# First modulation slot issued ahead of all else, recurrence masks loaded as bytes, positions worked on behind that slot

## The reference

```python
c_act = jax.nn.silu(c)
for l in range(DEPTH):                                  # DEPTH = 2
    mod = c_act @ w_mod[l] + b_mod[l]                   # (2048) @ (2048, 6144)
    shift, scale, gate = jnp.split(mod, 3, axis=-1)
    h = rmsnorm(x, norm_gain[l]) * (1.0 + scale[:, None, :]) + shift[:, None, :]
    proj = h @ w_in[l]
    ...
    att = sparse_attention(..., positions, rel_bias)    # bias = rel_bias[t5_bucket(pos_q - pos_k)]
    ...
    x = x + gate[:, None, :] * y
# second block: hgrn2_chunked over the rows, with causal masks inside each chunk
```

## Time and profile before

| | |
|---|---|
| median of 3 runs | 1891.88 us (1891.06 to 1892.19) |
| the profiled execution, its own time | 1894.75 us |
| its span in the profile | 1892.9 us |
| TensorE busy | 1851.9 us (98%) |
| VectorE, ScalarE, GpSimd busy | 71%, 52%, 11% |
| TensorE's share of the chain that ended last | 92% |
| mean granted TensorE clock | 0.988 |

### The profile page before, as it was taken

The page is one execution under the profiler, slowest core; times in us unless marked ns, Lnnn a source line. Parts: engine busy times, 40 slices in busy tenths (PEclk is TensorE's granted clock), DMA queues, the critical chain, the costliest instruction groups (busy, mean ns, idle before and its releaser), DMA issues.

```text
span 1892.9 us, 23983 instructions
## 1 busy us (share of the span) xinstructions
PE 1851.9 (98%) x9008; PEld 1535.2 (81%) x9008; DVE 1352.2 (71%) x1950; ACT 991.6 (52%) x1359; POOL 201.8 (11%) x256
## 2 busy tenths in 40 slices
PE   5989999999999999999999999999999999999997
PEld 3778788888888878888888888888888888888886
DVE  5988999989987778857765544487775456665555
ACT  6664555446446445544654644566665444444464
POOL 0000002100000000210000000044431020031001
PEclk9879999999999999999999999999999999999999
DMA  9998978975986986744465555654445555556552
GB/s 332 363 345 299 335 253 290 314 242 172 328 299 231 360 276 222 244 157 156 125 223 180 190 188 198 196 164 153 154 160 173 188 191 178 185 186 252 178 191 98
DMA packets 211825, 424.28 MB, mean 224 GB/s; under 512 B 7681, under 2 KB 12557, under 8 KB 210317
## 3 DMA queue, kind: packets, MB, share of 16 engines
q1 hardware_dynamic: 209788, 415.18, 64.6%
q10 hardware_dynamic: 1936, 7.76, 1.0%
HBM read 418.70 MB, written 4.21 MB: 223 GB/s over the span
## 4 chain that ended last, share of the span: by engine, by line
PE 92%; ACT 3%; DMA 2%; DVE 2%; issue 1%; SPq 0%; DVEq 0%; POOLq 0%; POOL 0%; ACTq 0%
PE acc L684 27%; PE acc L686 27%; PE acc L685 27%; DMA raw<-in_w_in 1%; PE sps L1075 1%; DVE scr L2076 1%; PE tps L725 1%; ACT w_hi L1414 1%; DMA xres<-in_x 1%; PE tps L765 1%; PE sps L790 0%; PE sps L892 0%; PE sps L893 0%; PE sps L996 0%; PE tps L988 0%
## 5 line engine op out<-in xcount | busy, mean ns | idle before, releaser
L1855 DVE TENSOR_TENSOR w_lo<-raw,w_hi 128x1024 fp32r<-128x1024 f32 (+1 forms) x580 | 720.8, 1249 | 461.3 <-ACT w_hi L1242 459.2
L1242 ACT ACTIVATE w_hi<-raw 128x1024 fp32r<-128x1024 f32 (+1 forms) x580 | 606.9, 1051 | 771.6 <-PE acc L686 693.8
L684 PE MATMUL acc<-w_hi,ht_hi 128*128 128x512 f32 (+1 forms) x2304 | 910.2, 395 | 0.5 <-issue 0.4
L686 PE MATMUL acc<-w_hi,ht_lo 128*128 128x512 f32 (+1 forms) x2304 | 894.1, 388 | 0.0
L685 PE MATMUL acc<-w_lo,ht_hi 128*128 128x512 f32 (+1 forms) x2304 | 892.3, 387 | 0.0
L686 PEld LDWEIGHTS acc<-w_hi,ht_lo 128*128 128x128 f32 x2304 | 432.4, 188 | 90.4
L684 PEld LDWEIGHTS acc<-w_hi,ht_hi 128*128 128x128 f32 x2304 | 432.9, 188 | 86.8 <-issue 2.6
L685 PEld LDWEIGHTS acc<-w_lo,ht_hi 128*128 128x128 f32 x2304 | 433.3, 188 | 83.4
L1987 DVE SCALAR_TENSOR_TENSOR scr<-raw,vcol,scr 128x512 f32<-128x512 f32 x154 | 110.9, 762 | 5.1 <-DVE w_lo L1855 0.5
L2076 DVE SCALAR_TENSOR_TENSOR scr<-raw,vcol,scr 128x1024 f32<-128x1024 f32 x56 | 68.2, 1279 | 6.9 <-DMA raw<-in_w_mod 6.9
L1987 DVE SCALAR_TENSOR_TENSOR proj<-raw,vcol,proj 128x512 f32<-128x512 f32 x70 | 52.3, 788 | 1.9
(11 more groups left out here) (304 smaller groups left out, 1480.3 us busy)
## 6 DMA issues: line engine op xcount, KB each, us to landing
raw<-in_w_in SPq DMA_DIRECT2D x208, 1024.0 KB, 5.1
raw<-in_w_mod SPq DMA_DIRECT2D x64, 1024.0 KB, 6.2
raw<-in_w_mod SPq DMA_DIRECT2D x64, 512.0 KB, 6.7
raw<-in_w_out SPq DMA_DIRECT2D x32, 1024.0 KB, 5.2
raw<-in_w_o SPq DMA_DIRECT2D x16, 1024.0 KB, 5.1
raw<-in_w_ple_gate SPq DMA_DIRECT2D x16, 1024.0 KB, 5.1
raw<-in_w_b_out SPq DMA_DIRECT2D x8, 1024.0 KB, 5.1
raw<-in_w_a_out SPq DMA_DIRECT2D x8, 1024.0 KB, 5.0
```

The source lines that it names most:

```text
L684: pe.matmul(o, hi_m, w_hi[:, slot, u, 0:width], start=start, stop=False)
L686: mm = pe.matmul(o, lo_m, w_hi[:, slot, u, 0:width], start=False, stop=stop)
L1242: act.activation(w_hi[:, x % SPL, :, 0:width], raw[:, j, 2 * (x % halves):2 * (x % halves) + 2, 0:width], ACT.Copy).then_inc(hi_ready, 1)
L1855: dve.tensor_tensor(w_lo[:, x % SPL, :, 0:width], raw[:, j, 2 * (x % halves):2 * (x % halves) + 2, 0:width], w_hi[:, x % SPL, :, 0:width]. ...
```

## The change

SP issues `mod_pair(0, 0)` first, then `consts` and `c`, then `mod_pair(0, 1)`. `levels` is handed over as an array of bytes, is loaded straight into `lvm`, and its transfer stands after the four quarters. VectorE's copy into `lvm` goes; a wait for the masks is put ahead of the recurrence. VectorE's work on positions moves from ahead of the first slot's `modulate` to behind it.

```diff
-    return k, lv
+    return k, lv.astype(np.uint8)
...
+            mod_pair(0, 0)
             sp.dma_start(kst[:, :], consts).then_inc(s_const, 16)
             vector_rows("c", c, s_c)
-            for j in range(2):
-                mod_pair(0, j)
+            mod_pair(0, 1)
             sp.dma_start(xres[:, :, :], x_rows).then_inc(s_x, 16)
...
             for j in range(2, RAW):
                 mod_pair(0, j)
-            sp.dma_start(scr[:, 5376:6016], levels.rearrange("p n t -> p (n t)")).then_inc(s_levels, 16)
...
+            sp.dma_start(lvm[:, :, :], levels).then_inc(s_levels, 16)
             for l in range(DEPTH):
...
-            dve.wait_ge(s_pos, 48)
-            dve.tensor_copy(prow, prow_i)
-            link(dve.tensor_copy(pcol, pcol_i))
...
+            def distances():
+
+                dve.wait_ge(s_pos, 48)
+                dve.tensor_copy(prow, prow_i)
+                link(dve.tensor_copy(pcol, pcol_i))
...
-            def bound_and_levels():
+            def bound_ratio():
                 dve.wait_ge(vec_ready, 2)
                 lp = v2("lb_param_2", 0, NH)
                 dve.tensor_tensor(lb_t[:, 0, :], lp, lp, ALU.subtract).then_inc(lb_stats, 1)
-                dve.wait_ge(s_levels, 16)
-                dve.tensor_copy(lvm[:, :, :], scr[:, 5376:6016].rearrange("p (n t) -> p n t", t=P))
-
-            dve.wait_ge(vec_ready, 1)
...
             dve.wait_ge(mod_summed, m_free.next(2))
+            dve.wait_ge(vec_ready, 1)
             for u in range(2):
                 modulate(0, 0, u)
+            distances()
...
                 if col == GATES:
+                    dve.wait_ge(s_levels, 16)
                     link(dve.memset(hat, 0.0))
```

More of the change, by code:

```diff
@@ L1945, in _ @@
             dve.memset(rb_diag, 0.0).then_inc(rb_zeroed, 1)
-            dve.wait_ge(s_pos, 48)
-            dve.tensor_copy(prow, prow_i)
-            link(dve.tensor_copy(pcol, pcol_i))
[L1949 to L1954, removed]
+            def distances():
+                dve.wait_ge(s_pos, 48)
+                dve.tensor_copy(prow, prow_i)
+                link(dve.tensor_copy(pcol, pcol_i))
+                for m in range(M):
+                    o, q = (slice(0, S), slice(0, S)) if m == 0 else (slice(S, 384), slice(P, S))
+                    r = dve.tensor_scalar(rel[:, o], prow[:, q], pcol[:, m:m + 1], None, ALU.subtract)
+                r.then_inc(rel_ready, 1)
+                dve.wait_ge(rel_ready, 1)
+                dve.tensor_scalar(bucket, rel, 0.0, float(EXACT), ALU.max, ALU.min).then_inc(clip_ready, 1)
             def buckets():
@@ L2100, in _ @@
                     if i == 0 and j == 6:
-                        bound_and_levels()
+                        bound_ratio()
                 dve.wait_ge(raw_read, own.ahead(0))
```

## The result

The changed kernel takes 1897.28 us (median of 6, 1896.07 to 1899.51) against 1891.59 for the one before (median of 6, 1891.01 to 1894.64): a ratio of 1.0027, 95% interval 1.0016 to 1.0037, so 3.0 to 7.0 us slower. A second set of runs gave 1.0026 (1.0016 to 1.0036). The forecast was 1893.2, with a range up to 1896.4.

The account below looks back on a forecast made before the run. TensorE is 98% busy, so only the head before full matmuls could move, paced by ScalarE's chain: +1.24 us for late squares, masks and copy 0, rounded to +1.3, giving 1893.2 us, range 1890.6 to 1896.4.

Parts of the forecast that it names:

- The bound and the way a delay is passed on: Head before full matmuls: ScalarE's chain sets `w_hi` at 41.77; the stream's earlier gain is lost as idle DMA.
- One for one: Head: what ScalarE's chain loses or gains before 41.77 us moves the end of the kernel equally.
- Masks and VectorE's copy: Stream and VectorE in the head: 0.83 us less stream and 0.49 us less copy, both worth nothing.
- S: Time VectorE can start the first slot, needing the slot and silu(c): taken as 8.2 us, bounds 6.7 and 12.4.
- the middle estimate: First slot lands at 7.7 us and `c` at 8.35, so VectorE can start the slot at 8.95.
- The price of S = 6.96 and beyond: ScalarE's squares: past 6.96 us they wait for signs, not x; a start at 8.2 costs 1.24 us.
- Signs start at S + 2.47: ScalarE's signs follow the first slot's two instructions (1.42 us) and the positions work (1.05 us).
- The buckets: VectorE, behind the signs: about 1.4 us later, from 16.79 to 18.2, with the third slot's wait as cover.
- Rival 3: Head: `c` held behind the slot until 10.2 or more, costing 3.8 us, up to 1897.3 at S = 12.4; chance 0.09.
- Rival 1: Head: no net effect, S at or under 7.2, signs end under cover of x; 1891.6 to 1892.2; chance 0.15.
- rival 2: Head: the stream's gain reaches the end, -1.5 us, 1890.4, if ScalarE's chain does not set 41.77; chance 0.10.
- Rival 4: TensorE's clock behind the head: low stretch changes length, 2.8 us less or more, 1889.1 to 1896.0; chance 0.06.

Follow-up runs that it names:

- held and ahead: Changed kernel with GpSimd's 3.60 us copy started only after VectorE clips the distances, and positions back ahead of the first slot: 1.0002 against the kernel before.
- changed kernel, again: The changed kernel, unaltered, timed once more against the kernel before on the same chip: 1.0026, +4.8 us.
- copy held: Changed kernel with a small identity tile made first and GpSimd's 3.60 us copy started only after VectorE clips the distances: 1.0014, +2.5 us against the kernel before.
- behind only: Kernel before with only VectorE's positions work moved behind the first slot; transfer order and masks as before: 1.0010, +1.9 us against the kernel before.

## Why the prediction was wrong

**The bound and the way a delay is passed on: right in kind.** ScalarE's squares set `w_hi`; in all fourteen profiles `w_hi` stands 24.6 us behind the squares to 0.05. The stream's gain was lost at 45 to 50, as said. "One for one" to the end is neither confirmed nor excluded: over the eight runs with late squares (from "held and ahead" to "changed kernel, again", 26.5 us of lateness in all) the medians gained 21.6, so 0.8 us for each, and the ratios give 23.3, so 0.9. The first set has 5.7 us for 5.31. Each of these times is uncertain by 1.7 us to either side. The first full matmul came 2.7 us later than in the first profile of the kernel before, and 3.7 to 4.8 later than in the second; it stands 116.3 to 119.0 us behind the squares in the fourteen profiles.

**Masks and VectorE's copy: right.** No effect found.

**S, the start of the first slot: mis-sized.** I took 8.2 and measured 9.93 and 10.16; the middle estimate was 8.95. The order of events was right: silu(c) is what it waits for. The constants took 9.09 - 1.82 = 7.3 us to be seen, `c` 7.0. SP's own issues also grew, `c` from 0.42 to 0.97. The pace was lower too: from 3 to 5 us the changed kernel moved 249 to 279 GB/s, where the estimates took 1 MB in 2.59 us. What held it there no run shows. By the prediction's own sum S = 9.93 puts the squares at 20.12 in place of 18.4, so this term was short by 1.7 us.

**The price of S = 6.96 and beyond: wrong by a term that was missing.** This is the step that failed, and the larger one. "Signs start at S + 2.47" took 1.42 us for the two instructions of the slot. They took 3.96. I had followed GpSimd's copy to 11.1 us for what waits for it, and had not asked what it does to VectorE beside it, though the estimate itself put both in the same stretch. So signs start at S + 4.93 = 14.86, 2.46 later than S alone would have it. The two terms together, 1.7 and 2.5, make up, to 0.1, the 4.07 us between the squares' forecast place of 18.41 and their measured 22.48.

Put in the order in which the runs take them away, the lateness of the squares is: GpSimd's copy beside VectorE 2.20 (changed kernel again, less copy held); positions behind the slot 2.01 (less held and ahead); positions landing late 1.03 (what is left). These add up to 5.24. In time the same steps are 2.4, 2.4 and 0.1 us, each with an uncertainty of over 1.

The last share depends on that order. With the positions behind the slot, as in the changed kernel, VectorE comes to them at 13.81 and no longer waits for their landing; what holds the head there is the start of the slot, and so `c`. The other way round the runs say so: from the kernel before to "behind only" 2.03 for the place of the positions, from there to "copy held" 1.01 (the slot starts at 10.34 in place of 9.31, since it waits for silu(c); the masks differ too, which moved nothing), and from there to the changed kernel 2.20 for the copy. In the changed kernel the third step is therefore the late `c`, and the late positions take its place only where they stand ahead of the slot.

The buckets were misread, without consequence: signs that start at 10.7 in place of 8.37 move them by 2.3 us and not by 1.4. They moved by 6.49, and the third slot's work lost its cover, as the prediction had named for signs over 3 us late.

A page states what I missed. The Trainium skill, "SBUF — State Buffer", section "SBUF: two separate sides", says that VectorE and GpSimd share one pair of ports. Whichever starts first has it for its whole instruction, and the other waits in full; on VectorE's side this holds for instructions in a two-port mode, and for those with two inputs in that memory against a GpSimd instruction that reads there. The trace agrees as to the waiting: 3299 ns against 741 for the same instruction, ending at 13.23, just behind GpSimd's copy at 12.69. In which mode VectorE ran no row shows.

The rule that the prediction held against the rows, 2.0 us plus bytes over 436 GB/s, stands in the Trainium skill, "DMA: Bandwidth & Descriptors", section "Anatomy of one DMA", for transfers that GpSimd issues. Those here are SyncE's, so the 4.2 us of `c` do not test it.

**Rivals.** Rival 3 had the right sign and size, and 0.09 of the chance. Its place was half right: `c` was late and held the slot, but only to 9.35 and not to 10.2; and the largest single part, 2.20 us, came from the copy, which it did not have. That the time came near its 1897.3 is luck: it had that figure for S = 12.4. Rival 1 fell with S, rival 2 with `w_hi`. Rival 4, the clock, works against the loss and is small. The low stretch ended at 141.84 before, and at 142.83 in the changed kernel, 5.7 and 4.0 us behind the first full matmul. In the fourteen profiles it is 8 to 14 matmuls long, 3.5 to 6.1 us, in no order of lateness (8 in "behind only", 14 in "copy held"). Each matmul in it takes 0.43 us from start to start in place of 0.23. So the whole spread is worth 1.2 us, and between the kernel before (13 and 12 matmuls) and the changed one (9 and 10) it gives back 0.4 to 0.8. What sets its length no run shows.

## What to carry to other kernels

When a transfer is moved, follow every engine that wakes up on it, and ask what that engine's work then runs beside: GpSimd's copy was harmless only because it had run while VectorE waited. With 1 MB put first, the small transfers behind it came late, and so did small ones on another queue. Before optimizing a stream, find what it waits for when all its slots are full: here a chain on ScalarE, so neither fewer bytes nor an earlier first slot could pay.

## What was not expected of the hardware

- In the rows here GpSimd's copy and VectorE's casts, products with one tensor and products with two exclude each other instruction by instruction: a cast of 0.28 us took 3.43 to 3.56, and a copy of 3.60 us in eight pieces took 5.61. With the copy held, an instruction of VectorE that reads two tensors took 4.62 us in place of 1.28, and the copy 4.59 in place of 3.60:

```profile
14.13 4.62 DVE L2075 SCALAR_TENSOR_TENSOR scr<-raw,vcol,scr 128x1024 f32<-128x1024 f32 x1
```

- The three transfers of positions on ACT's queue (128 KB and two of 0.5 KB) had all landed at 9.5 to 9.65 in place of 7.2 to 7.7 when SP's queue began with 1 MB, though nothing on ACT's queue had changed. The two small ones lost the most: 5.1 us to landing before, 6.9 with the order alone changed, against 4.2 and 5.1 for the large one.
- A slow stretch at the start of the stream did not go away with another order, but it moved and was shallower: from 3.5 to 5 us the changed kernel carried 236 to 262 GB/s at a DMA share of 0.71 to 0.80, the last of these windows being:

```profile
4.50:5.00 0.50, 0.00 (x0) 0.00 (x0) 0.00 (x0) 0.00 (x0) 0.00 (x0) 1.00 0.78 262
```
